# Two layers and 32 experts on one core: where the second layer's weights are split, and which expert weights come earlier

## The chip, the cores and the metric

The kernel runs on one core of one Trainium2 chip. Its time is device microseconds (us) of one execution. The core has TensorE (PE; its weight loads are a row of their own, PEld), VectorE (DVE), ScalarE (ACT), GpSimd (POOL) and SyncE (SP), which issues the DMAs here. A DMA is spread over 16 DMA engines.

## The reference, cut to what matters

256 tokens of width 1024 pass through two layers. Everything is float32.

- Layer one: norm, one wide projection, a windowed mean, a stick-breaking attention, a cross attention over a memory, three sigmoid gates, an output projection with a residual, then a feed-forward part of width 2816.
- Layer two: norm, `h @ w_in` (columns for two attentions, an index and two gates), block attention `a`, attention `b` on the 64 best-scored positions, `sigmoid(ga) * (o_a @ w_proj_a) + sigmoid(gb) * (o_b @ w_proj_b)`, then `@ w_out` and the residual.
- A mixture of experts behind it:

```
g_sel = argmax(h @ w_group + b_group)                 # one of 4 groups per token
e_logit = (h @ w_expert + b_expert)[group g_sel]      # 8 experts in it
top_p, top_i = top_k(softmax(e_logit), 2)             # 2 experts per token
hid = silu(xb @ w1[e]) * (xb @ w3[e]);  y = hid @ w2[e]
out = x + sum of gate * y;  then a last rms_norm with g_final
```

Each of the 32 experts has three matrices of 2 MB (w1, w3: 1024 x 512, w2: 512 x 1024), and all of them are read: about 201 MB of the 309 MB that the kernel moves.

## The kernel before, in words

**Units.** The dense weights of both layers come in 96 pieces ("units", numbered u) of 1 MB (128 partitions x 2048 floats). To keep float32 accuracy each is split: ACT copies it to a rounded high part (`w_hi`, line 1526), DVE subtracts that from the raw unit and writes the low part (`w_lo`, line 1867), and PE makes three products (lines 927 to 929). Raw, high and low parts have three places each, used in turn by u % 3. The raw places are `ring`, slots 1 to 3 of a 12-slot `arena` (one slot holds 1 MB). Unit u is loaded (`load`, line 685) once the low part of unit u - 3 is written. Layer two's units are `kiwi` (u = 65), `qi`, `kb`, `qb`, `vb`, `ka`, `qa`, `va`, eight `gate2`, four merges (`w_proj_a`, `w_proj_b`, u = 88 to 91) and four `out2` (92 to 95).

**The queue of DMAs.** SP issues all loads in one written order; each `wait_ge` holds back all that stands behind it. Expert weights are put between the units and behind them, each as soon as its place is free. `expert_load` (line 746) loads a whole matrix, `half_load` (753) a half of expert 0's, `chunk_load` (757) some chunks of a matrix (w1 and w3 have 8 chunks of 256 KB, w2 has 4 of 512 KB).

**Places of experts.** Expert e = 0 uses `even_w` (arena slots 8-9, the place of `x_both`, slots 4-5), e = 1 `odd_w` (w1 in slots 10-11, w3 in slots 0-1, w2 in slots 2-3), e = 2 `third_w` (where the last units are split), e = 3 `fourth_w`; expert 4's w1 has `next_w1`, its w3 follows into even w1's place. So odd w3's second half and w2 lie in the raw places of units, and wait for the last units.

**From the last unit to the experts.** After unit 95 PE computes the last routing logits (line 1234), then runs `CHOICE_WARM` = 7 products on ones whose result is not used (`keep_warm`, line 1117), then spreads the final norm's gain over the partitions (line 1348; ACT copies it to `final_row`, line 1798). DVE meanwhile chooses the experts (up to line 2402, `route_sel`). PE waits for that and for the first copy (`final_taken`), ranks the tokens (1354, 1356), gathers them for a quad of four experts (`first_collect`, 1380) and starts expert 0: w1 and w3 (line 1454), the gates' spread (1417), w2 (1480), and the sum into the tokens (`add_to_tokens`, 1433). The signals `e_w1_half` (expert 0's w1 half used), `e_w1`, `e_up` (w3 used) and `e_y` (w2 used) free the places, for which SP waits.

**Quads.** Quads 0 and 1 are written out on PE, quads 2 to 7 are a loop (`pe.Fori`, line 1490) with even and odd places alone. ACT has quad 0 written out and loops over 1 to 7. In the loop the last expert's w2 comes in two pieces (SP line 844), 1.5 MB and 0.5 MB; PE waits for the second ahead of its last quarter. Then the last norm follows (lines 1830 to 1838, 2504 to 2527).

Of the kernel before, what the change touches and what calls it, by code (L numbers as in the profile page):

```python
# [51 lines left out]
CHOICE_WARM = 7  # L52
# [231 lines left out]
def layers_kernel(nc, a, table, windows, out):  # L284
# [121 lines left out]

    def split_place(u):

        return split_at + 2 * SLOT_B * (u % 3)
# [50 lines left out]
    final_row = moe("final_row", [P, D])  # L460
# [95 lines left out]
    next_in = sem("next_w1_in")  # L556
# [4 lines left out]
    e_w1, e_w1_half = sem("e_w1"), sem("e_w1_half")  # L561
# [116 lines left out]
    def _(sp):  # L678
        def load(u):
            if u >= 3:  # L680
                sp.wait_ge(lo_ready, u - 2)
            kc, cols = units[u]["kc"], units[u]["cols"]
            dst = ring[:, u % 3, 0:kc * cols].rearrange("p (c n) -> p c n", c=kc)
            for c0, c1, src in units[u]["src"]:
                sp.dma_start(dst[:, :, c0:c1], src).then_inc(landed[u % 3], 16)
# [73 lines left out]
        for u in range(S2 + 3 * (NF - 2), U):  # L759
# [16 lines left out]
            load(u)  # L776
            if u == first["kiwi"]:
# [20 lines left out]
        expert_load(2, third_w, 2, in_third3[2])  # L798
        sp.wait_ge(route_T, 4)
# [122 lines left out]
    def _(pe):  # L922
# [8 lines left out]
        def unit(u):  # L931
# [3 lines left out]
            lo = w_lo[:, s, 0:kc * cols].rearrange("p (c n) -> p c n", c=kc)  # L935
# [409 lines left out]
        for half in range(2):  # L1345
            for j in range(4):
                c = 44 + 4 * half + j
                last = mm(ps[:, 4 + half, P * j:P * j + P], vec[:, c:c + 1].to_broadcast([P, P]), ident, start=True,
                          stop=True)
            last.then_inc(final_spread, 1)  # L1350
        pe.wait_ge(route_sel, 1)
        pe.wait_ge(final_taken, 1)

# [5 lines left out]
        def quad_body(q):  # L1359
# [24 lines left out]
            if not looped and q == 0:  # L1384
                pe.wait_ge(hot_part, 2)
                first_collect(4, (0, 1), xg_half)
                pe.wait_ge(final_taken, 2)
# [50 lines left out]
            for e in range(QUAD):  # L1438
                places, landing, arrived = place_of(e)
                done = pe.snap(e0 + e) if looped else e0 + e  # L1440
                for n in range(2):
                    if not looped and e == 0 and (q == 0 or n == 1):
                        pe.wait_ge(first_half[n], 16 * (q + 2 - n))
                    if not looped and (q, e, n) == (0, 1, 1):
                        pe.wait_ge(second_up_half, 16)
                    pe.wait_ge(landing[n], arrived[n])
                    for c in range(KC):
# [3 lines left out]
                        elif e == 0 and n == 0 and c % 4 == 0:  # L1451
                            pe.wait_ge((xg_part, xg_ready)[c // 4], q + 2)
                        for g in range(4):
                            last = mm(ps[SLOTS * g:SLOTS * g + SLOTS, 6, P * n:P * n + P],  # L1454
                                      xg[:, c, SLOTS * e:SLOTS * e + SLOTS], places[n][:, c, P * g:P * g + P],
                                      start=c == 0, stop=c == KC - 1, tile_position=(0, SLOTS * g))
                        if not looped and (e, n, c) == (0, 0, KC // 2 - 1):
                            if q == 0:
                                last.then_inc(e_w1_half, 1)
# [29 lines left out]
        quad_body(1)  # L1489
        with pe.Fori(2, n_pass * (EXPERTS // QUAD)) as q:  # L1490
            quad_body(q)
# [3 lines left out]
    def _(act):  # L1495
# [24 lines left out]
        def split_one(u):  # L1520
# [5 lines left out]
            fn(w_hi[:, u % 3, 0:n], ring[:, u % 3, 0:n], ACT.Copy).then_inc(hi_ready, 1)  # L1526
# [269 lines left out]
        for half in range(2):  # L1796
            act.wait_ge(final_spread, half + 1)
            fn(final_row[:, 512 * half:512 * half + 512], ps[:, 4 + half, :], ACT.Copy).then_inc(final_taken, 1)
# [4 lines left out]
        def quad_body(q):  # L1803
            e0 = act.snap(q * QUAD) if not isinstance(q, int) else 0
            act.wait_ge(xg_half, q + 2)
            if isinstance(q, int):
# [749 lines left out]
```

## Time and profile before

| | us |
|---|---|
| median of 3 runs (lowest, highest) | 1057.65 (1056.35, 1058.83) |
| the profiled execution | 1058.77 |
| its span, first to last instruction | 1056.7 |
| PE busy in it | 918.5 (87%) |
| DVE, ACT busy | 498.0, 385.2 |

How to read it: the span is cut in stretches, and each stretch has its own limit. "Idle before, releaser" names what ended an engine's idle time; "issue" is idle time for which the profile shows no event that was waited for. "us to landing" of a DMA runs from its issue on SP to the last of its pieces. PEclk is the granted TensorE clock as a share of 2.4 GHz. Packets of the queues named "instruction" fetch an engine's code. The profiled execution is 2.1 us longer than its span and 1.1 us longer than the median.

### The profile page before, as it was taken

How to read it: one execution, taken by the hardware profiler on the slowest of the kernel's cores; microseconds unless marked ns; L12 is line 12 of the kernel's file. 1: busy time of each engine (PE TensorE's matmuls, PEld its weight loads, DVE VectorE, ACT ScalarE, POOL GpSimd, SP SyncE). 2: the span in 40 equal slices, each digit the busy share in tenths (PEclk: the TensorE clock that was granted, in tenths of full speed). 3: DMA queues.
4: the chain of work that ended last, by engine and by line, in shares of the span. 5: the costliest groups of instructions: out<-in, count | busy, mean ns of one | idle time of the engine just before them, and what ended most of it. 6: DMA issues, size and time to landing. Idle time of an engine off the chain costs nothing.

```text
span 1056.7 us, 22572 instructions
## 1 busy us (share of the span) xinstructions
PE 918.5 (87%) x9950; PEld 761.6 (72%) x9950; DVE 498.0 (47%) x807; ACT 385.2 (36%) x553; POOL 21.6 (2%) x24
## 2 busy tenths in 40 slices
PE   9999999999999999999999997787757667575764
PEld 8998887888888888988777885665635546463643
DVE  5646768677676767889887650111100101010101
ACT  5445766464444446756666340000000000000001
POOL 0000002110000000000000000000000000000000
PEclk9999999999999999999999999999898978888987
DMA  9864445545655575665447999999999999999994
GB/s 328 293 194 159 165 136 175 163 150 190 213 162 195 199 254 162 198 202 163 160 170 286 389 401 426 425 425 421 427 427 427 430 429 427 429 427 428 431 428 200
DMA packets 89455, 309.49 MB, mean 293 GB/s; under 512 B 7940, under 2 KB 48696, under 8 KB 76600
## 3 DMA queue, kind: packets, MB, share of 16 engines
q1 hardware_dynamic: 88768, 308.40, 75.8%
q8 instruction: 42, 0.69, 0.3%
q10 hardware_dynamic: 632, 0.29, 0.1%
q14 instruction: 13, 0.11, 0.0%
HBM read 307.63 MB, written 1.05 MB: 292 GB/s over the span
## 4 chain that ended last, share of the span: by engine, by line
PE 62%; DMA 28%; DVE 4%; issue 3%; ACT 1%; POOL 0%; SPq 0%; DVEq 0%; ACTq 0%
DMA arena<-in_w 27%; PE ps L927 12%; PE ps L929 11%; PE ps L928 11%; PE ps L1037 7%; PE ps L1454 7%; PE ps L1041 4%; PE ps L1480 2%; DMA arena<-in_w_in 1%; PE ps L1219 1%; PE ps L1371 1%; DVE w_split L1867 1%; PE ps L1433 1%; PE ps L1417 1%; PE ps L1207 0%
## 5 line engine op out<-in xcount | busy, mean ns | idle before, releaser
L1867 DVE TENSOR_TENSOR w_split<-arena,w_split 128x2048 fp32r<-128x2048 f32 (+1 forms) x69 | 157.2, 2288 | 29.9 <-ACT w_split L1526 29.4
L1454 PE MATMUL ps<-arena,xg 128*32 128x128 f32 x2688 | 104.8, 318 | 74.0 <-DMA arena<-in_w 66.7
L2474 DVE TENSOR_TENSOR hid<-silu_e,ps 128x128 f32<-128x128 f32 x32 | 12.1, 378 | 311.7 <-ACT silu_e L1814 311.7
L1526 ACT ACTIVATE w_split<-arena 128x2048 fp32r<-128x2048 f32 x70 | 132.8, 1901 | 63.7 <-PE ps L929 53.1
L1454 PEld LDWEIGHTS ps<-arena,xg 128*32 128x32 f32 x2688 | 89.3, 129 | 91.8 <-DMA arena<-in_w 79.4
L927 PE MATMUL ps<-w_split,x_both 128*128 128x512 f32 x256 | 102.1, 399 | 0.6 <-DVE expo_pair L2117 0.6
L929 PE MATMUL ps<-w_split,x_both 128*128 128x512 f32 x256 | 99.8, 390 | 0.0
L928 PE MATMUL ps<-w_split,x_both 128*128 128x512 f32 x256 | 99.8, 390 | 0.0
L1814 ACT ACTIVATE silu_e<-ps 128x128 f32<-128x128 f32 x32 | 8.9, 277 | 240.1 <-PE ps L1454 240.1
L1037 PE MATMUL ps<-x_both,w_split 128*128 128x512 f32 x352 | 83.9, 390 | 0.1
L1480 PE MATMUL ps<-arena,hid_T 128*32 128x256 f32 x896 | 61.5, 415 | 24.1 <-DMA arena<-in_w 21.8
L1037 PEld LDWEIGHTS ps<-x_both,w_split 128*128 128x128 f32 x352 | 65.2, 188 | 13.3 <-issue 0.3
L927 PE MATMUL ps<-x_both,w_split 128*128 128x256 f32 (+1 forms) x256 | 73.0, 285 | 0.9 <-ACT p_tok L1561 0.8
L928 PE MATMUL ps<-x_both,w_split 128*128 128x256 f32 (+1 forms) x256 | 72.3, 283 | 0.0
L929 PE MATMUL ps<-x_both,w_split 128*128 128x256 f32 (+1 forms) x256 | 72.3, 283 | 0.0
L927 PE MATMUL ps<-w_split,o_hi 128*128 128x512 f32 (+1 forms) x176 | 68.0, 387 | 0.5 <-DVE gates L2090 0.5
L928 PE MATMUL ps<-w_split,o_hi 128*128 128x512 f32 (+1 forms) x176 | 67.0, 381 | 0.0
L1877 DVE TENSOR_TENSOR w_split<-arena,w_split 128x2048 fp32r<-128x2048 f32 x24 | 55.0, 2292 | 25.4 <-ACT w_split L1536 24.2
L929 PE MATMUL ps<-w_split,o_lo 128*128 128x512 f32 (+1 forms) x176 | 66.9, 380 | 0.0
L1480 PEld LDWEIGHTS ps<-arena,hid_T 128*32 128x32 f32 x896 | 30.3, 116 | 49.7 <-issue 30.9
L927 PEld LDWEIGHTS ps<-w_split,x_both 128*128 128x128 f32 x256 | 48.1, 188 | 14.2 <-issue 3.0
L929 PEld LDWEIGHTS ps<-w_split,x_both 128*128 128x128 f32 x256 | 48.0, 188 | 10.3
(325 smaller groups left out, 1462.0 us busy)
## 6 DMA issues: line engine op xcount, KB each, us to landing
arena<-in_w SPq DMA_DIRECT2D x65, 2048.0 KB, 26.3
arena<-in_w_in SPq DMA_DIRECT2D x41, 1024.0 KB, 5.2
even_w<-in_w SPq DMA_DIRECT2D x12, 2048.0 KB, 27.0
arena<-in_w_ffn_in SPq DMA_DIRECT2D x22, 1024.0 KB, 5.1
third_w<-in_w SPq DMA_DIRECT2D x6, 2048.0 KB, 16.9
arena<-in_w_ffn_out SPq DMA_DIRECT2D x11, 1024.0 KB, 4.9
arena<-in_w_out SPq DMA_DIRECT2D x8, 1024.0 KB, 6.2
extra_w<-in_w SPq DMA_DIRECT2D x4, 2048.0 KB, 19.0
```

Source lines behind the costliest of these rows:

```text
L927: mm(dst, l_hi, r_hi, start=start, stop=False)
L928: mm(dst, l_hi, r_lo, start=False, stop=False)
L929: return mm(dst, l_lo, r_hi, start=False, stop=stop)
L1037: mm(ps[:, bank + n, :], hi[:, c, P * n:P * n + P], x_both[:, c, :, :].rearrange("p a b -> p (a b)"), start=c == 0, stop=False)
L1041: last = mm(ps[:, bank + n, 0:T], lo[:, c, P * n:P * n + P], x_hi[:, c, :], start=False, stop=c == KC - 1)
L1219: mm(o[:, 0:T], v[:, 0, :], r[:, 0:T], start=True, stop=False)
L1454: last = mm(ps[SLOTS * g:SLOTS * g + SLOTS, 6, P * n:P * n + P], xg[:, c, SLOTS * e:SLOTS * e + SLOTS], places[n][:, c, P * g:P * g + P], ...
L1480: last = mm(ps[SLOTS * g:SLOTS * g + SLOTS, 7, 0:UC], hid_T[:, SLOTS * b:SLOTS * b + SLOTS], places[2][:, b, UC * g:UC * g + UC], start=b ...
L1526: fn(w_hi[:, u % 3, 0:n], ring[:, u % 3, 0:n], ACT.Copy).then_inc(hi_ready, 1)
L1867: v.tensor_tensor(w_lo[:, u % 3, 0:n], ring[:, u % 3, 0:n], w_hi[:, u % 3, 0:n].bitcast(F32), ALU.subtract).then_inc(lo_ready, 1)
L1877: v.tensor_tensor(w_lo[:, s, :], ring[:, s, :], w_hi[:, s, :].bitcast(F32), ALU.subtract)\
L2474: v.tensor_tensor(hid[:, :].rearrange("p (b i) -> p i b", b=4), silu_e[:, :].rearrange("p (i b) -> p i b", b=4), ps[:, 6, P:2 * P].rearran ...
```

## The change

1. From unit 65 on the raw unit lands in the place of its low part, and DVE subtracts in place. There are four such places in turn by u % 4: the three of `w_lo` and `ring_low` (arena slot 3). For one turn in four the raw unit lands in arena slot 3 itself, as for the others it lands in its `w_lo`. Unit u is now loaded once unit u - 4 has been computed (`unit_done`) and the high part of u - 3 is written. Arena slots 1 and 2 are free of units from there on.
2. The 2 MB of expert 1 that lie in slots 1 and 2 are loaded there: w3's second half behind unit `ka` (74), w2's first half behind unit `qa` (76). W2's second half (slot 3) waits for unit 92.
3. `spare_w` (4 KB per partition, 0.5 MB) takes the first two chunks of expert 4's w3, loaded behind unit 95. The next two chunks go where expert 0's first two w1 chunks were, once these are used (`e_w1_part`, after chunk 1 instead of chunk 3). The other half goes as before, at `e_w1`. `final_row` moves to `next_w1`'s place.
4. The spread of the final gain moves on PE from ahead of the ranking to behind quad 1, and its copies on ACT likewise; ACT has quad 1 written out too. `CHOICE_WARM` goes from 7 to 23.
5. In the looped quads PE runs `keep_warm(10)` ahead of the last expert's w1 and again ahead of its w3.

```
-CHOICE_WARM = 7
+CHOICE_WARM = 23
+LAST_WARM = 10
+    ring_low = nc.alloc_sbuf_tensor_at("ring_low", [P, UNIT], F32R, offset=arena_at + 3 * SLOT_B)
+    raw_low = [nc.alloc_sbuf_tensor_at(f"raw_low{i}", [P, UNIT], F32, offset=split_at + 2 * SLOT_B * i + SLOT_B)
+               for i in range(3)]
+    def low_place(u):
+        if u < KW:
+            return w_lo[:, u % 3, :]
+        turn = (u - U) % 4
+        return w_lo[:, turn - 1, :] if turn else ring_low[:, :]
+    def raw_place(u):
+        if u < KW:
+            return ring[:, u % 3, :]
+        turn = (u - U) % 4
+        return raw_low[turn - 1][:, :] if turn else ring[:, 2, :]
...
         def load(u):
-            if u >= 3:
+            turn = (u - U) % 4
+            if u >= KW + 4:
+                sp.wait_ge(unit_done, u - 3)
+                sp.wait_ge(hi_ready, u - 2)
...
+            elif u >= 3:
                 sp.wait_ge(lo_ready, u - 2)
...
             load(u)
+            if u == first["ka"]:
+                sp.wait_ge(lo_ready, KW)
+                chunk_load(1, odd_w, 1, slice(KC // 2, KC), landed_w[1][1])
+            elif u == first["qa"]:
+                chunk_load(1, odd_w, 2, slice(0, 2), second_up_half)
...
         expert_load(1, odd_w, 0, landed_w[1][0])
-        sp.wait_ge(lo_ready, U - 2)
-        chunk_load(1, odd_w, 1, slice(KC // 2, KC), landed_w[1][1])
+        sp.wait_ge(unit_done, U - 3)
+        chunk_load(1, odd_w, 2, slice(2, 4), landed_w[1][2])
         sp.wait_ge(unit_done, U - 2)
         expert_load(2, third_w, 0, in_third3[0])
-        sp.wait_ge(lo_ready, U)
-        expert_load(1, odd_w, 2, landed_w[1][2])
         sp.wait_ge(unit_done, U - 1)
         expert_load(2, third_w, 1, in_third3[1])
         sp.wait_ge(unit_done, U)
         expert_load(2, third_w, 2, in_third3[2])
+        sp.dma_start(spare_w[:, :, :], sources[1][:, 4, 0:2, :]).then_inc(spare_in, 16)
...
         expert_load(3, fourth_w, 1, in_fourth[1])
-        for half, landing in ((0, first_half[1]), (1, landed_w[0][0])):
-            sp.wait_ge((e_w1_half, e_w1)[half], 1)
-            chunk_load(4, next_w, 1, slice(KC // 2 * half, KC // 2 * half + KC // 2), landing)
+        sp.wait_ge(e_w1_part, 1)
+        sp.dma_start(even_w[0][:, 0:2, :], sources[1][:, 4, 2:4, :]).then_inc(first_half[1], 16)
+        sp.wait_ge(e_w1, 1)
+        chunk_load(4, next_w, 1, slice(KC // 2, KC), landed_w[0][0])
...
         keep_warm(CHOICE_WARM, 5)
-        for half in range(2):
-            for j in range(4):
-                ... (the spread of the final gain, 8 products; now behind quad_body(1))
         pe.wait_ge(route_sel, 1)
-        pe.wait_ge(final_taken, 1)
...
                 for n in range(2):
+                    if looped and e == QUAD - 1:
+                        keep_warm(LAST_WARM, 5)
...
         quad_body(1)
+        (the spread)
+        pe.wait_ge(final_taken, 2)
         with pe.Fori(2, n_pass * (EXPERTS // QUAD)) as q:
```

## Rows read from the trace of the kernel before

**Rows 1.** The page: busy tenths in 40 slices of PE and DMA.

```profile
PE   9999999999999999999999997787757667575764
DMA  9864445545655575665447999999999999999994
```

**Rows 2.** Windows: busy us (instructions) of each engine, PEclk, DMA share, GB/s.

```profile
400.00:440.00 40.00, 39.27 (x310) 36.24 (x309) 32.21 (x49) 28.07 (x46) 1.96 (x3) 1.00 0.57 183
628.00:632.00 4.00, 4.00 (x115) 3.38 (x109) 2.28 (x8) 0.88 (x2) 0.00 (x0) 1.00 1.00 354
760.00:1035.00 275.00, 181.98 (x3752) 138.74 (x3744) 23.66 (x63) 17.92 (x47) 0.00 (x0) 0.87 1.01 428
```

**Rows 3.** The chain that ended last, 1000 to 1057: start, us, what.

```profile
1011.19 2.00 PE ps L1454 x64
...
1013.21 27.31 DMA arena<-in_w
...
1040.56 3.46 PE ps L1454 x64
...
1045.13 1.98 PE ps L1480 x32
```

**Rows 4.** Timeline of ACT: start, us, engine, line, operation; the split of unit 83.

```profile
504.54 1.91 ACT L1526 ACTIVATE w_split<-arena 128x2048 fp32r<-128x2048 f32 x1 [2.95 <-PE ps L929]
```

**Rows 5.** Timeline of SP's issues, 586 to 627.

```profile
586.26 0.34 SPq L746 DMA_DIRECT2D extra_w<-in_w  x1
...
604.90 8.09 SPq L746 DMA_DIRECT2D third_w<-in_w  x2
615.66 0.33 SPq L746 DMA_DIRECT2D extra_w<-in_w  x1
623.99 3.43 SPq L757 DMA_DIRECT2D arena<-in_w  x2
```

**Rows 6.** DMA issues at 558.69, 615.66, 627.09 and 1020.14: KB each, us to landing.

```profile
even_w<-in_w SPq DMA_DIRECT2D x1, 1024.0 KB, 5.0
...
extra_w<-in_w SPq DMA_DIRECT2D x1, 2048.0 KB, 12.3
...
arena<-in_w SPq DMA_DIRECT2D x1, 1024.0 KB, 8.9
...
arena<-in_w SPq DMA_DIRECT2D x1, 512.0 KB, 25.3
```

**Rows 7.** Timeline around the choice of experts.

```profile
615.77 1.81 PE L1117 MATMUL ps<-ones 128*128 128x128 f32 x14
617.41 1.95 PE L1348 MATMUL ps<-tab,vec 128*128 128x128 f32 x16
618.45 0.20 DVE L2402 TENSOR_SCALAR chosen<-left_e 128x64 f32<-128x64 f32 x1
```

**Rows 8.** Windows ahead of and in the last expert's w1 (as rows 2).

```profile
1032.80:1035.60 2.80, 0.00 (x0) 0.00 (x0) 0.00 (x0) 0.38 (x1) 0.00 (x0) 1.00 1.02 432
1035.60:1038.60 3.00, 2.65 (x64) 2.19 (x64) 0.00 (x0) 0.00 (x0) 0.00 (x0) 0.69 0.95 397
```

**Rows 9.** Windows between idle times of PE called issue, and one loop pass (814.03).

```profile
642.30:648.80 6.50, 3.90 (x128) 3.63 (x128) 0.00 (x0) 0.38 (x1) 0.00 (x0) 1.00 0.98 416
705.55:708.20 2.65, 2.17 (x28) 1.14 (x28) 0.00 (x0) 0.38 (x1) 0.00 (x0) 1.00 1.00 427
814.03:873.47 59.44, 40.46 (x804) 31.05 (x808) 5.21 (x14) 3.83 (x10) 0.00 (x0) 0.85 1.01 429
```

**Rows 10.** The chain, 620 to 720: an idle time called issue.

```profile
704.59 0.96 issue
```

**Rows 11.** DMA queues, 558 to 760, then 760 to 1050: packets, MB, share of 16.

```profile
q8 instruction: 22, 0.36, 0.7%
...
q1 hardware_dynamic: 8393, 120.03, 97.3%
q14 instruction: 1, 0.01, 0.0%
```

More of the change, by code:

```diff
@@ L404, in layers_kernel @@
     gates2 = temp("gates2", [P, 16, T])
+    KW = next(u for u, x in enumerate(units) if x["name"] == "kiwi")
+    ring_low = nc.alloc_sbuf_tensor_at("ring_low", [P, UNIT], F32R, offset=arena_at + 3 * SLOT_B)
[11 more added lines that the diff above has]
+        return raw_low[turn - 1][:, :] if turn else ring[:, 2, :]
     def split_place(u):
@@ L1452, in quad_body @@
                             pe.wait_ge((xg_part, xg_ready)[c // 4], q + 2)
+                        source = places[n][:, c, :]
+                        if not looped and (q, e, n) == (1, 0, 1) and c < KC // 2:
+                            source = (spare_w if c < 2 else even_w[0])[:, c % 2, :]
                         for g in range(4):
                             last = mm(ps[SLOTS * g:SLOTS * g + SLOTS, 6, P * n:P * n + P],
-                                      xg[:, c, SLOTS * e:SLOTS * e + SLOTS], places[n][:, c, P * g:P * g + P],
+                                      xg[:, c, SLOTS * e:SLOTS * e + SLOTS], source[:, P * g:P * g + P],
                                       start=c == 0, stop=c == KC - 1, tile_position=(0, SLOTS * g))
+                        if not looped and (q, e, n, c) == (0, 0, 0, 1):
+                            last.then_inc(e_w1_part, 1)
                         if not looped and (e, n, c) == (0, 0, KC // 2 - 1):
                             if q == 0:
-                                last.then_inc(e_w1_half, 1)
                                 first_collect(7, (4, 5), xg_done)
@@ L1489, in _ @@
         quad_body(1)
+        for half in range(2):
+            for j in range(4):
+                c = 44 + 4 * half + j
+                last = mm(ps[:, 4 + half, P * j:P * j + P], vec[:, c:c + 1].to_broadcast([P, P]), ident, start=True,
+                          stop=True)
+            last.then_inc(final_spread, 1)
+        pe.wait_ge(final_taken, 2)
         with pe.Fori(2, n_pass * (EXPERTS // QUAD)) as q:
@@ L1803, in quad_body @@
         def quad_body(q):
-            e0 = act.snap(q * QUAD) if not isinstance(q, int) else 0
+            e0 = act.snap(q * QUAD) if not isinstance(q, int) else q * QUAD
             act.wait_ge(xg_half, q + 2)
-            if isinstance(q, int):
+            if isinstance(q, int) and q == 0:
                 fn(xg[:, 2:4, :].rearrange("p a b -> p (a b)"), ps[:, 5, 0:2 * P], ACT.Copy).then_inc(xg_part, 1)
@@ L1823, in _ @@
         n_pass = act.value_load(passes_i[0:1, 0:1], min_val=1, max_val=T // SLOTS)
-        with act.Fori(1, n_pass * (EXPERTS // QUAD)) as q:
+        quad_body(1)
+        for half in range(2):
+            act.wait_ge(final_spread, half + 1)
+            fn(final_row[:, 512 * half:512 * half + 512], ps[:, 4 + half, :], ACT.Copy).then_inc(final_taken, 1)
+        with act.Fori(2, n_pass * (EXPERTS // QUAD)) as q:
             quad_body(q)
```

33 lines of the change are left out of this document (17 added, 16 removed).

## The prediction, made before the change was run

> **What bounds the kernel now.** The page's slices come first [rows 1]: PE is at nine tenths or more up to slice 23, about 610 us, and then falls to 7 and 4; the DMA row does the reverse, 4 to 6 before and 9 from slice 22 on. So there are two kernels. Up to the last unit PE sets the pace and the DMA engines have room (share 0.57 from 400 to 440). From 760 to 1035 they move 428 GB/s at share 1.01 and PE is busy 182 of 275 us [rows 2]: 2 MB (2.10 million bytes) take 2.10 / 0.428 = 4.9 us, and a load more or less in this stage is worth that. The seam between them is the place to look at. From 628 to 632 the rate is 354, not 428 [rows 2]: the queue nearly runs out just after the experts are chosen, because all places are full. The end is read from the chain [rows 3]: the last w3 lands at 1040.5, PE takes 3.46 us for its 64 instructions (the same 64 took 2.00 at 1011), and w2 follows at 1045.13.
>
> **The change part by part.** The sum is made against the profiled execution, 1058.77 us (span 1056.7). That is 1.1 above the median of the runs, 1057.65, and the result is carried over to the median by that difference.
>
> *Units loaded later.* Unit u - 3's low part no longer lets unit u in; unit u - 4's end on PE does. The tightest split in the middle is that of unit 83: ACT began it at 504.54, having waited 2.95 us for PE [rows 4], and its load would now go out one unit before, where a 1 MB load onto a free queue takes 5.0 [rows 6]; a unit takes about 1.05 / 0.183 = 5.7 us by the rate from 400 to 440 [rows 2]. It is just in time, and PE needs the unit only two units later, 11 us, for two splits of some 2 us each. At the other end unit 95 goes out with the wait that now releases the first expert load behind it, at 586.26 [rows 5], and ahead of that in the queue: landing near 592. PE wants it when unit 94 ends, at 604.90, where third w3 is issued [rows 5]. Its cover is PE's own work on units 93 and 94; were the load 8 us late, PE would wait. Cost 0; bounds 0 and +1 us.
>
> *2 MB of expert 1 early.* Two 1 MB loads go out near 445 and 458, into a queue at share 0.57 [rows 2]: free. What is late next? If the queue stayed full, the end would come 4.9 us sooner. It doesn't. All that is issued up to 615.66 landed at 615.66 + 12.3 = 628.0 [rows 5, 6]. Without 2 MB the queue has run dry by the time unit 95 ends: third w2, the 0.5 MB of `spare_w` and fourth w3 (4.5 MB, 11.0 us) can't flow before 604.90 + 8.09 - 0.33 = 612.7 [rows 5] plus about 2.5 (5.0 for 1 MB [rows 6], less 2.45 of transfer), so they end near 626. Then 0.5 MB at `e_w1_part`, and nothing until `e_w1`. The gain ends at a new gap, and what decides is when the `e_w1` load goes out and lands.
>
> *The ranking later.* Before, 7 warm products are 14 PE instructions in the 1.64 us from 615.77 to 617.41, and the 8 products of the spread end at 619.36 [rows 7]. After, 23 warm products stand there: 46 instructions at 1.64 / 14 = 0.117 are 5.4 us, at the 0.111 of the fastest stretch 5.1; PE is free at about 620.9 to 621.1. DVE had its choice at 618.65 [rows 7]: the warm products, not the choice, hold the ranking. It comes 1.6 us later, and the chain from there to expert 0's w1 is serial. All instructions count: 16 products more, 8 gone. The spread itself, 1.95 us on PE and two copies on ACT, moves behind quad 1. PE then waits for ACT's second copy before quad 2, and nobody waits for PE but loads that have several others ahead of them in the queue (a load at the end takes 25.3 us to land for 4.9 of its own [rows 6]): 0, bound +0.5.
>
> *The `e_w1` load.* Before: issued at 627.1 (the second of two from 623.99 on, 3.43 us in all), landed 8.9 later, at 636.0 [rows 5, 6]. After: issued at 627.1 + 1.6 = 628.7 onto a dry queue, landed 5.0 later, at 633.7 if nothing else is on the engine. That is 2.3 sooner. An instruction packet may fall on the last engine: 22 packets had 0.7% of 16 engines' 202 us, 1.03 us each [rows 11]. So 1.3 to 2.3 sooner, and 0.8 if a packet holds up half as much again (1.5, an estimate for what waits behind it); I take 1.6. The 1 MB loaded in the gap (`spare_w` and the `e_w1_part` chunk) is what buys this. From here the queue is never empty again, as before, and each landing follows the last by 4.9 us. Bounds: -2.4, and +1.2 if the gap costs as much as the bytes bring in.
>
> *The warm products in the loop.* Ahead of the last w1 PE stood idle from 1032.8 to 1035.6, and w1 then ran at a granted clock of 0.69, which is a mix of 1.2 and 2.4 GHz [rows 8]; w3 behind it took 3.46 us instead of 2.00. Ten products (2.2 us at the full clock) fit in either gap: w3 lands at 1040.5 [rows 3], w1 4.9 before it, at 1035.6. If they keep the clock up, w3 ends 1.46 us sooner. Not all of it counts: w2's last 0.5 MB land at 1020.14 + 25.3 = 1045.4 [rows 6], the 1.5 MB ahead of them 1.2 before, at 1044.2. W2 would start at 1044.2 instead of 1045.13, and its last quarter is then ready. Gain 0.9; bounds 1.4 and a loss of 2.9 (below).
>
> *Code.* Nothing else is on the path: `spare_w`'s wait is met long before, ACT's written-out quad runs in slack of many us.
>
> Sum: -1.6 - 0.9 = -2.5. 1058.77 - 2.5 = 1056.3 on the scale of the profiled execution, 1055.2 on that of the median.
>
> **A page's rule against this change.** PE's instructions come in blocks, and the trace shows where they end. Between two idle times of PE called issue it ran 128 + 128 instructions [rows 9], and a packet of the instruction queue is 0.36 MB / 22 = 16 KB [rows 11]: 256 instructions are one block. One such idle time ends at 705.56 [rows 10]; 56 instructions of PE and PEld and two more of its queue later, at 708.2, the looped quad starts [rows 9]. A pass has 804 + 808, with its branch 1613. It starts at 58 in a block and ends at 1671, in the seventh (1536 to 1792). After 760 there is no packet of that queue, though the loop is passed five times more [rows 11]: seven blocks, and the next one fetched ahead, all stay. After the change the 16 added warm products put the start at about 121 (four instructions each), the 20 in the loop add 80, and the end is at 121 + 1693 = 1814: 22 instructions into an eighth block, with a ninth fetched ahead. Whether nine fit, no row shows.
>
> The Trainium skill (Runtime: NRT & Kernel Launch, Instruction fetch mechanics) says that PE's instruction memory is a FIFO of 128 KiB, 2048 instructions, refilled in 16 KiB blocks. By that rule eight blocks are all, the ninth drives out the first, and each pass fetches anew. The block size agrees with the trace; the depth isn't shown beyond eight.
>
> **The rivals.**
> 1. *The loop's code no longer stays.* For it: the count above. Against it: nothing in the rows but that eight blocks do fit. Price: 9 blocks in each of 5 passes, 45 packets of 1.03 us beside full queues. Spread over 16 engines that is 2.9 us on each, over eight 5.8, and with the estimate of 1.5 us for a packet's whole delay 8.5. The end waits for the slowest engine. I take 8.5: 1055.2 + 8.5 = 1063.7. It decides once the body reaches an eighth block.
> 2. *The gap takes everything.* PE reaches `e_w1` 1.6 later and the dry queue restarts no earlier than the old one flowed, with the tail's 0.9 alone: 1056.8. For it: the old queue still moved 354 GB/s in the gap [rows 2], 83% of the full rate, and the ranking is 1.6 us late. Against: the old load took 8.9 us, a free queue takes 5.0.
> 3. *The warm products are in the way.* If the clock stays at 1.2 GHz in the last expert, ten take 4.5 us: w1 3.3, warm 4.5 from 1035.66 end at 1043.4, 2.9 behind the landing of w3. Then 1057.65 - 1.6 + 2.9 = 1059.0. For it: 0.69 in [rows 8]. Against: PE is then hardly idle ahead of w1, and the clock was at full before it fell there.
> 4. *The whole 2.5 MB pays*, with no gap: -6.1 - 0.9, 1050.6. For it: only that the bytes are free. Against: all places are full until expert 0's w1 is used.
>
> **How the numbers follow.** My forecast has 0.50, rival 1 0.22, rival 2 0.14, rival 3 0.07, rival 4 0.07. A measurement of this kernel tells a change of some 0.2%, 2.1 us, from none: faster is below 1055.5. The forecast's own range is 1053.4 to 1057.2, two thirds of it on the faster side: 0.34; with rival 4, 0.41. Same: 0.16 of the forecast, rival 2, and 0.03 of rival 3, 0.33. Slower: rival 1 and the rest of 3, 0.26. The range goes from 1052.6 to 1064.5: it leaves out rival 4 and the upper part of rival 1.
>
> **What would show it.** The ranking on PE at about 621 instead of 619.3, right behind the warm products; a dip in the DMA rate near 613 and a deeper one, to nearly nothing, between 626 and 631; the `e_w1` load issued near 628.7 and landed by 635; every later landing of the same load earlier by about 1.6; in the tail w3's 64 instructions in 2.0 us and the last w2 starting on its landing, not on `hid_T`. Wrong it is if the 16 KB instruction packets go on after 760 (rival 1), if the last landing is not earlier than 1045.4 (rival 2), if the clock around 1036 to 1044 is 0.5 with PE busy at 1040.5 (rival 3), or if PE shows new idle time before 612 that ends with a DMA or with `w_split`.

## The result: 1082.6 us, 2.4% slower

The changed kernel took 1082.60 us in the median of 5 runs (1080.34 to 1083.93), the kernel before 1057.63 beside it (5 runs, 1056.35 to 1058.83). The ratio is 1.0238, 95% interval 1.0227 to 1.0250. The forecast was 1055.2 with a range up to 1064.5: wrong in its sign, and outside the range.

The profiled execution of after took 1083.93 us with a span of 1082.0, 25.3 above the span of before. Its page, the busy tenths of PE and DMA, the granted clock, and the row of the instruction queue (packets, MB, share of 16 engines):

```profile
PE   9999999999999995999999998788766776766665
...
PEclk9999999999999996999999999999798988988899
DMA  9864444546565535666447989999999999999994
...
q8 instruction: 88, 1.44, 0.5%
```

Against [rows 1] two things are new. PE has a hole in slice 15, about 406 to 433 us, where it had nine tenths; its clock falls there too. And the instruction queue moved 88 packets instead of the 42 of the kernel before (the same row is shown for e12 below).

The windows that answer to [rows 2] (the last one starts a little later, since the stream does), and the hole by itself:

```profile
400.00:440.00 40.00, 26.81 (x178) 23.67 (x178) 20.33 (x34) 20.75 (x34) 1.97 (x3) 0.79 0.62 206
403.00:417.00 14.00, 1.14 (x10) 0.94 (x9) 3.46 (x7) 4.71 (x10) 0.55 (x1) 0.71 1.02 355
...
761.00:1051.00 290.00, 202.77 (x4088) 165.36 (x4091) 25.41 (x68) 18.55 (x48) 0.00 (x0) 0.90 1.01 425
```

PE lost 12.5 us of its 39.3 in the first window. In the last one the queues are as full as before and the rate is 425 instead of 428 GB/s.

**The 25.3 us by stretch.** All times are from one profiled execution of each kernel. "Landing" is the time at which the slowest of the 16 DMA engines has finished a load. The fourth column is a mended kernel, explained under e12.

| stretch | before | after | e12 |
|---|---|---|---|
| last unit done by PE | 612.64 | 628.58 (+15.9) | 613.20 |
| from there to the landing of the `e_w1` load | 23.37 | 21.27 (-2.1) | 20.78 |
| from there to the last landing | 409.43 | 421.73 (+12.3) | 410.88 |
| from there to the end of the span | 11.26 | 10.4 (-0.9) | 10.4 |

The second and the fourth line are the gains that the forecast counted (1.6 and 0.9). The first it priced at nothing. The third holds the spread, priced at nothing too, and the loop's code, which was no term of the sum but rival 1.

**The first loss: 15.9 us at the feed-forward's end.** The timeline of SP in after (start, us until the last of the group, line, what is loaded), and of the waits from 390 to 440 (engine, operation, what it waited for: us in total, times, longest):

```profile
397.76 0.99 SPq L717 DMA_DIRECT2D raw_low<-in_w_in  x2
398.79 0.89 SPq L789 DMA_DIRECT2D next_w<-in_w  x1
400.10 0.34 SPq L720 DMA_DIRECT2D gain_row<-in_g_ffn  x1
403.20 1.80 SPq L717 DMA_DIRECT2D raw_low<-in_w_in  x2
```

```profile
ACT w_split L1569 <- DMA raw_low<-in_w_in: 18.1, 2, 9.1
PEld ps L1160 <- DVE h L2003: 13.8, 2, 13.0
PE ps L1160 <- DVE h L2003: 13.2, 2, 12.9
DVE y_tok L2026 <- ACT junk L1734: 10.1, 1, 10.1
```

The text on the change above says that a unit from 65 on waits for the computing of unit u - 4. For the first four of them that isn't so. Their wait is a branch of `load` of its own:

```
            elif u >= KW and turn:
                sp.wait_ge(unit_done, max(v for v in range(KW) if v % 3 == turn - 1) + 1)
                sp.wait_ge(hi_ready, u - 2)
            elif u >= KW:
                sp.wait_ge(lo_ready, KW)
                sp.wait_ge(hi_ready, u - 2)
```

Units 65 and 66 are the first whose raw weights land in a low place. Such a place is free only when PE is done with the unit that has it: units 63 and 64, at 397.7 and 403.2. Before, the same two loads went out once the low parts of units 62 and 63 were split, at 381.4 and 385.3, 16 and 18 us sooner. Behind the first of them SP issues 2 MB of `next_w` and a gain row, and unit 66 follows those. ACT works in order. It waits 9.1 us for unit 65 and 8.9 for unit 66, and the feed-forward's norm stands behind that split on ACT:

```profile
402.04 1.11 ACT L1569 ACTIVATE w_split<-raw_low 128x1088 fp32r<-128x1088 f32 x1 [9.15 <-DMA raw_low<-in_w_in]
412.07 1.91 ACT L1569 ACTIVATE w_split<-raw_low 128x2048 fp32r<-128x2048 f32 x1 [8.91 <-DMA raw_low<-in_w_in]
413.89 0.58 ACT L1734 ACTIVATE junk<-ps 128x512 f32<-128x512 f32 x1
```

DVE waits for `junk`, PE for `h`, idle for 12.86 us until 416.92, and then the granted clock is 0.81 from 417 to 440, a mix of the two levels. Unit 65 is done at 429.6 instead of 413.6. From there to the last unit nothing is lost and nothing regained (199.0 us in both kernels).

**The second loss: the loop's code is fetched again in every pass.** The timeline of PE at a loop head, and its waits from 774 to 1069:

```profile
771.65 1.15 PE L1461 MATMUL ps<-y_part,gate_T 32*128 32x256 f32 x16 [0.50 <-ACT y_part L1859]
778.45 2.92 PE L1400 MATMUL ps<-one_hot,n3g 128*128 128x128 f32 x12 [5.65 <-issue]
```

```profile
PE ps L1400 <- issue: 27.0, 5, 5.7
...
PE ps L1445 <- issue: 8.4, 5, 1.9
PE ps L1489 <- issue: 8.2, 5, 2.0
```

L1400 is the first operation of the looped quad. Five times PE has no instruction there for 5.4 us in the mean, and ten times more, for 1.7 in the mean, further on in the loop; in e2, whose code stays, it has no such idle time. The queue in that stretch, 44 packets where [rows 11] has none:

```profile
q8 instruction: 44, 0.72, 1.0%
```

This is the first rival: the loop starts at 121 of one block, ends 22 instructions into its eighth, and is fetched anew in each of five passes, nine packets a pass. PE's own stalls did not slow the loads: the first DMA engine (of the 16, the one that is done first with a load) finishes the last load 318.18 us after its first landing of this stage (742.00 to 1060.18), exactly as before (720.49 to 1038.67). The packets cost more: the slowest engine ends 11.4 us after the first instead of 6.8. At the stage's start that distance was 1.9 us against 5.2 before, so it grew by 9.5 instead of 1.6. Of the fifteen profiles here only those of after and e1, the two with 88 packets, end with 11.4; the other thirteen have 2.3 to 6.9. That it is the packets which hold up the slower engines is inferred from this; no row shows on which engine a packet ran.

**The third loss: the queue runs dry at the loop's start.** PE's timeline between quad 1 and the loop, against [rows 9, 10]:

```profile
725.24 1.15 PE L1461 MATMUL ps<-y_part,gate_T 32*128 32x256 f32 x16 [0.47 <-ACT y_part L1859]
726.31 2.05 PE L1529 MATMUL ps<-tab,vec 128*128 128x128 f32 x16
729.32 3.83 PE L1400 MATMUL ps<-one_hot,n3g 128*128 128x128 f32 x32 [0.95 <-ACT final_row L1867]
```

The spread and ACT's second copy put 3.0 us between quad 1 and the loop. The first load that the loop releases went out 21.2 us later than before (735.1 against 713.9): 15.9 from the units, 1.7 from the ranking, 3.0 from the spread, and 0.6 that none of them explains. What was left in the queue landed only 17.6 us later (732.9 against 715.3 on the first engine), so the first engine's landings lie 9.1 us apart there, where before they lay 5.2 apart and elsewhere in the stream lie 4.9. The slowest engine's lie 6.95 apart instead of 4.89, so 2.1 us are lost there.

### The profile page after: what moved, and what is told of

It is laid out like the page before. It is cut to its first block, busy times and chain, and to the rows that moved or that the text cites. A ratio compares the mean times of both kernels' runs of the same rounds, so it can differ in the third digit from the quotient of the medians.

```text
span 1082.0 us, 23140 instructions
## 1 busy us (share of the span) xinstructions
PE 944.1 (87%) x10222; PEld 791.4 (73%) x10222; DVE 497.9 (46%) x807; ACT 385.6 (36%) x553; POOL 21.7 (2%) x24
## 4 chain that ended last, share of the span: by engine, by line
PE 68%; DMA 18%; issue 6%; DVE 5%; ACT 2%; POOL 0%; SPq 0%; DVEq 0%; ACTq 0%
DMA arena<-in_w 16%; PE ps L964 12%; PE ps L965 11%; PE ps L966 11%; PE ps L1074 7%; PE ps L1489 6%; PE ps L1516 5%; PE ps L1078 4%; PE ps L1400 3%; PE ps L1445 1%; DMA arena<-in_w_in 1%; PE ps L1461 1%; PE ps L1154 1%; DMA raw_low<-in_w_in 1%; PE ps L1256 1%
## 5 line engine op out<-in xcount | busy, mean ns | idle before, releaser
L1489 PE MATMUL ps<-arena,xg 128*32 128x128 f32 x2672 | 86.0, 277 | 30.7 <-DMA arena<-in_w 16.5
L1569 ACT ACTIVATE w_split<-arena 128x2048 fp32r<-128x2048 f32 x46 | 87.8, 1912 | 44.5 <-PE ps L966 37.3
L1489 PEld LDWEIGHTS ps<-arena,xg 128*32 128x32 f32 x2672 | 74.2, 111 | 40.3 <-DMA arena<-in_w 20.5
L964 PE MATMUL ps<-w_split,x_both 128*128 128x512 f32 x256 | 102.1, 399 | 0.6 <-DVE expo_pair L2161 0.6
L966 PE MATMUL ps<-w_split,x_both 128*128 128x512 f32 x256 | 99.8, 390 | 0.0
L1911 DVE TENSOR_TENSOR w_split<-arena,w_split 128x2048 fp32r<-128x2048 f32 x38 | 87.3, 2312 | 25.1 <-ACT w_split L1569 25.0
L965 PE MATMUL ps<-w_split,x_both 128*128 128x512 f32 x232 | 90.4, 390 | 0.0
L1074 PEld LDWEIGHTS ps<-x_both,w_split 128*128 128x128 f32 x352 | 65.2, 188 | 13.3 <-issue 0.3
L964 PE MATMUL ps<-x_both,w_split 128*128 128x256 f32 (+1 forms) x256 | 73.9, 288 | 0.9 <-ACT p_tok L1604 0.9
L965 PE MATMUL ps<-x_both,w_split 128*128 128x256 f32 (+1 forms) x256 | 73.2, 286 | 0.0
L964 PE MATMUL ps<-w_split,o_hi 128*128 128x512 f32 (+1 forms) x176 | 68.1, 387 | 0.5 <-DVE gates L2134 0.5
L1921 DVE TENSOR_TENSOR w_split<-arena,w_split 128x2048 fp32r<-128x2048 f32 x24 | 55.0, 2293 | 25.4 <-ACT w_split L1579 24.2
L966 PE MATMUL ps<-x_both,w_split 128*128 128x256 f32 x224 | 64.0, 286 | 0.0
L965 PE MATMUL ps<-w_split,o_hi 128*128 128x512 f32 (+1 forms) x168 | 63.9, 380 | 0.0
L1400 PE MATMUL ps<-one_hot,n3g 128*128 128x128 f32 x224 | 36.9, 340 | 28.3 <-issue 27.3
L964 PEld LDWEIGHTS ps<-w_split,x_both 128*128 128x128 f32 x256 | 48.0, 188 | 14.2 <-issue 3.3
## 6 DMA issues: line engine op xcount, KB each, us to landing
arena<-in_w SPq DMA_DIRECT2D x64, 2048.0 KB, 25.3
```

The costliest lines, as they stand in the source:

```text
L964: mm(dst, l_hi, r_hi, start=start, stop=False)
L965: mm(dst, l_hi, r_lo, start=False, stop=False)
L966: return mm(dst, l_lo, r_hi, start=False, stop=stop)
L1074: mm(ps[:, bank + n, :], hi[:, c, P * n:P * n + P], x_both[:, c, :, :].rearrange("p a b -> p (a b)"), start=c == 0, stop=False)
L1400: last = mm(ps[:, 4 + half, P * i:P * i + P], n3g[:, tb, 4 * half + i, :], one_hot[:, tb, :], start=tb == 0 and i == 0, stop=tb == 1 and i ...
L1569: fn(w_hi[:, u % 3, 0:n], raw_place(u)[:, 0:n], ACT.Copy).then_inc(hi_ready, 1)
```

## The experiments

Each kernel is the changed one with the edit shown. From e5 to e9 the kernel of e4 is the base (`CHOICE_WARM` at 7, and `KW` as in e4 unless another is given), for e10 and e11 it is that of e9. Times are medians with the ratio to the kernel before on the same chip.

**e1, the four low places from four units later.** With `KW` at 69 instead of 65 the feed-forward's end has three places again.

```
-    KW = next(u for u, x in enumerate(units) if x["name"] == "kiwi")
+    KW = next(u for u, x in enumerate(units) if x["name"] == "kiwi") + 4
```

> The change, but the four low places take raw units from unit 69 on instead of 65, so that units 65 to 68 are loaded as before the change. Theory A (in the change units 65 and 66 are let in by PE's end of units 63 and 64, 16 us later than before; ACT, which must split them in order, holds up the squares of the feed-forward's end, and PE stands still for 12.9 us): all of it goes, 1082.6 - 16 = 1066.6 us, and PE ends its last unit near 613 instead of 628.6. Rival (the raw unit in the low place, with the subtraction in place, is what is slow): some 27 of 31 units still do that, so it stays within 2 us of 1082.6.

1069.33 us (4 runs), ratio 1.0115 [1.0093, 1.0136]: 13.3 less. The last unit is done at 614.96, not 628.58; the instruction queue still has 88 packets. The first loss is shown, and that it is apart from the second. In this profiled execution 2.3 us of it stay.

**e2, seven warm products ahead of the ranking, and e3, none in the loop.** Both shorten PE's code, at different places: e2 puts the loop's end at 213 of its seventh block, e3 at 197 (offsets from 0, good to a few instructions).

```
e2:  -CHOICE_WARM = 23   +CHOICE_WARM = 7
e3:  -LAST_WARM = 10     +LAST_WARM = 0
```

> The change with 7 instead of 23 warm products ahead of the choice: PE's code ahead of the loop is 64 instructions shorter, the loop is the same. Theory B (the loop's end lies 22 instructions in an eighth block of 256, so with the block fetched ahead nine are wanted and eight stay): now the loop ends in its seventh block, no 16 KB instruction packets after the loop's first pass, 46 fewer in all, 8 us less for them and 1.6 us less for the earlier ranking: about 1073. Rival (the 20 warm products in each pass are what holds the loop up, by their own time): the packets may be as they are, and the time falls by the ranking's 1.6 us at most, 1081.

> The change without the 20 warm products in each pass of the loop: 80 instructions fewer in the loop, which then ends in its seventh block. Theory B: the repeated packets go, 8 us less, but the tail's 0.9 us come back: 1075.5. Rival (the warm products' own time): also lower, by what they take, so this run alone does not part the two; the pair with the run before it does. If neither holds, the repeated packets stay and the time is 1083.

e2: 1071.97 us (4 runs), 1.0137 [1.0115, 1.0158]. e3: 1073.63 us (4 runs), 1.0156 [1.0136, 1.0176]. Both have 42 packets and no idle time at a loop head. But e2 still has the 20 products of each pass and e3 the 23 ahead of the ranking, so the packets go with where the loop lies and not with the products by themselves. The waits of PE from 774 to 1045 in e2 are all for data:

```profile
PE ps L1489 <- DMA arena<-in_w: 39.1, 21, 2.9
PE ps L1516 <- DMA arena<-in_w: 23.8, 19, 1.9
PE ps L1489 <- DMA even_w<-in_w: 12.7, 8, 2.9
PE ps L1461 <- ACT y_part L1859: 2.0, 4, 0.5
```

e3 leaves the ranking and the spread as they are and gives 9.0 us back, although its tail is longer again (11.2 us from the last landing to the end). With those 0.85 the code's share is some 9.8 us, an estimate from one difference. e2 gives 10.6: the code, and the ranking 1.6 us sooner. In e2 no landing of the first engine lies more than 4.95 from the last at the loop's start, in e3 one is 7.5 away: the spread alone does not empty the queue there, the spread with the late ranking does. The late ranking without the spread was not run.

**e4, both mended**, `KW` at 69 and `CHOICE_WARM` at 7.

> Units from 69 on and 7 warm products. Theory: 16 + 8 + 1.6 us off, 1057.0 us, about the kernel before (1057.6): the 2 MB loaded early are worth little, because the queue then runs dry until expert 0's w1 is used, and what is left of the difference is the tail's 0.9 us less and a gap of the DMA engines at the loop's start (the spread behind quad 1) of some 2 us more. Rival (the early 2 MB pay in full once nothing is in the way): 4.9 us below that, 1052.

1058.62 us (10 runs), ratio 1.0008 [0.9998, 1.0019]; run again beside e12 (as e13) 1058.01 (11 runs), 1.0006 [0.9997, 1.0015]. Two edits take 24 of the 25 us away. After, e1, e2 and e4 are the four combinations of the two edits: `KW` is worth 13.3 us without the other edit and 13.4 with it, `CHOICE_WARM` 10.6 and 10.7 (after on another chip, where the kernel before took 1057.63 against 1057.24 here). The two losses add up and do not touch each other. What is left is "no change", where gains of some 3 us had been counted.

> The kernel of e4 again, on the same chip as e12, so that the two are compared there: 1058.0 to 1059.5 by its first run (1058.6). Theory: 2 to 3.5 above e12. Rival: equal to it.

**e5, e6 and e7, where the loop lies.** Is it the number of blocks, the length of the code, or an address? N small products ahead of the loop push it along without changing it.

```
+        for _ in range(N):          # 10 in e5, 12 in e6, 52 in e7
+            mm(ps[:, 6, 0:16], ones, ones[:, 0:16], start=True, stop=True)
         pe.wait_ge(final_taken, 2)
         with pe.Fori(2, n_pass * (EXPERTS // QUAD)) as q:
```

> The kernel of e4 (1058.6) with ten small products (16 columns) on PE ahead of the looped quad. Blocks of 256 instructions, counted from the idle times of PE at their ends: the loop now runs from 97 of block 35 to 253 of block 41, three instructions short of an eighth block. Theory (the loop's code stays as long as it lies in seven blocks): instruction packets as in e4 (42), none after the loop's first pass, 1058.5 to 1060. Rival (the larger code by itself, or the place of the loop's start, costs): some 2 to 4 us more than e4.

> The same with twelve products instead of ten: the loop ends 5 instructions into block 42, its eighth. Theory: the packets come back in every pass, about 88 in all, PE idles near 5.9 us at the head of every pass, and the time is 1058.6 + 8 = 1066 to 1069 for two products more. Rival (what cost in the kernel after was the number of warm products, not the block's border): as with ten products, 1059.

> The same with fifty-two products: the loop runs from 9 of block 36 to 165 of block 42, again in seven blocks, though it ends further on than with twelve. Theory: 42 to 44 packets, none after the first pass, and 1059 to 1062 (the forty products more are some 160 instructions in the gap ahead of the loop, up to 3 us). Rival (a fixed address or the whole length of the code decides): 88 packets or more, 1067 or more.

| kernel | loop, block and offset | packets | us, runs | ratio |
|---|---|---|---|---|
| e4 | 35:57 to 41:213 | 42 | 1058.62, 10 | 1.0008 [0.9998, 1.0019] |
| e5 | 35:97 to 41:253 | 42 | 1058.01, 10 | 1.0005 [0.9995, 1.0015] |
| e6 | 35:105 to 42:5 | 43 | 1058.90, 10 | 1.0020 [1.0002, 1.0037] |
| e7 | 36:9 to 42:165 | 43 | 1073.45, 4 | 1.0145 [1.0128, 1.0162] |
| after | 35:121 to 42:21 | 88 | 1082.60, 5 | 1.0238 [1.0227, 1.0250] |

Blocks are numbered over the whole program, and the places come from the instructions counted between the idle times at block ends; offsets count from 0 and are good to a few instructions. e6 is a miss of my theory. Its loop reaches offset 5 of an eighth block, and the profiled execution fetched nothing in the later passes. So a loop that touches eight blocks can stay. In after, whose loop runs 16 instructions further into the same block, all of them are fetched again; the nearest reading is that PE has by then asked for a ninth, which drives the first out. The times of the packets bear it out. The 43rd, by this count the first behind the eighth block, comes at 773.4 in after, at the end of the first pass and before the next begins at 778.4, and the refetch follows from 775.8 on. In e6 it comes at 1049.6, when the passes are over or nearly so. No run shows the point between 5 and 21 at which PE asks. e6's runs spread more than e5's (1056.6 to 1065.0 against 1056.3 to 1060.6), and whether some of them fetched again was not profiled.

The Trainium skill (Runtime: NRT & Kernel Launch, Instruction fetch mechanics) gives PE a FIFO of 128 KiB, filled in blocks of 16 KiB: eight blocks. By that rule e6 keeps its loop and after loses it as soon as a ninth block is fetched, and both traces agree. The same section of the Trainium skill calls the cost of a block's border mostly hidden. In this loop it was not: some 9 to 10 us.

e7 is a second miss, of price. Its code stays (43 packets, none in the later passes, though its loop ends further on than after's), so an address or the length of the program is not what decides. But its time is 15 us above e5. The timeline of PE in e7:

```profile
705.17 2.05 PE L1529 MATMUL ps<-tab,vec 128*128 128x128 f32 x16
707.06 19.53 PE L1533 MATMUL ps<-ones 128*128 128x16 f32 x104
726.43 5.75 PE L1400 MATMUL ps<-one_hot,n3g 128*128 128x128 f32 x32
```

Fifty-two products took 19.5 us, 0.19 for each of 104 instructions, where I had counted up to 3 us for forty of them. At the price of e5 (20 instructions in 2.30 us, 0.115 each) the 104 would be 12.0; the rest is the clock, granted at 0.57 in this stretch, a mix of 1.2 and 2.4 GHz near the lower:

```profile
707.10:726.50 19.40, 19.40 (x107) 19.40 (x105) 0.00 (x0) 0.60 (x1) 0.00 (x0) 0.57 0.56 235
```

The first load of the loop went out at 734.1, the queue ran dry (the first engine's landings lie 24.5 us apart), and 15.4 of the 17.2 us that the products take beyond those of e5 reached the end. That is the third loss in large: the start of the loop has some 2 us of slack.

**e8 and e9, the four low places from unit 72 and from unit 71.** In its profile e4's last unit is still 4.3 us late, in that of e13 3.0. Both profiles show the slowest of their kernel's runs (1061.28 of a median of 1058.62, 1062.23 of 1058.01), so the typical run may be less late.

```
e8:  ... if x["name"] == "kiwi") + 7
e9:  ... if x["name"] == "kiwi") + 6
```

> The kernel of e4 with the four low places from unit 72 on instead of 69. The first unit of the new order now takes the new place, not one whose unit is still to be used, and units 73 and 74 wait for units 69 and 70 (before: done at 437.5 and 444.3), no later than they used to. Theory (what e4 still loses, 4.3 us at the last unit, is loads 69 to 71 waiting for units 66 to 68): last unit done near 612.7, and 1054.5 to 1056, faster than the kernel before by some 2 us. Rival (e4's late last unit comes from elsewhere, the chip or the 2 MB beside the units): 1058 to 1059.

> The kernel of e4 with the four low places from unit 71 on (e4: 69, e8: 72). Worked out from the trace of before: each first load of the new order goes out when its place's last user is done or split, and lands 5.2 us later; against the start of its split in before that is 11.3 and 11.0 us late for units 65 and 66 in the kernel after, 3.1, 2.9 and 3.1 late for 69 to 71 in e4, 4.1 late for unit 72 in e8, and with the change at 71 only 3.1 late for unit 71. Theory (PE's lost time ahead of the last unit is ACT waiting in order for such a load): last unit done 612.7 to 614.7 instead of 617.0, time 1054.5 to 1057. Rival (the late last unit comes from elsewhere): 617 and 1058.6.

e8: 1059.32 us (10 runs), 1.0016 [1.0006, 1.0025], last unit 617.09. e9: 1060.53 us (6 runs), 1.0029 [1.0017, 1.0041], last unit 615.61. Neither helps; my theory's number for e8 was wrong, and the working for e9 (a load 3.1 us late) was right in the lateness and wrong in what it costs. The waits of e9 from 426 to 458, ACT's and then PE's:

```profile
ACT w_split L1569 <- DMA raw_low<-in_w_in: 2.9, 1, 2.9
ACT rope_turned L1587 <- PE ps L966: 2.8, 2, 1.7
...
PE ps L1363 <- ACT head_score L1803: 2.1, 1, 2.1
```

Two splits in a row wait for their loads, unit 71's for 2.9 us and unit 72's for 2.4, and `head_score` stands behind the second on ACT. The timelines of ACT, e9 and then before:

```profile
437.61 1.91 ACT L1569 ACTIVATE w_split<-raw_low 128x2048 fp32r<-128x2048 f32 x1 [2.87 <-DMA raw_low<-in_w_in]
...
444.36 1.91 ACT L1569 ACTIVATE w_split<-arena 128x2048 fp32r<-128x2048 f32 x1 [2.38 <-DMA arena<-in_w_in]
446.30 0.87 ACT L1803 ACTIVATE head_score<-ps 128x384 f32<-128x384 f32 x2
```

```profile
439.98 1.92 ACT L1526 ACTIVATE w_split<-arena 128x2048 fp32r<-128x2048 f32 x1
441.93 0.87 ACT L1760 ACTIVATE head_score<-ps 128x384 f32<-128x384 f32 x2
```

PE idles 2.1 us where before it had no idle time at all (unit 71 done at 454.10, before 451.12). In e4 and e8 the same wait is 1.7 and 2.0 us, and the granted clock from 445 to 450 is 0.73 in e8. At each of the three starts tried (69, 71, 72) some load changes from waiting for a split to waiting for a unit, and between 435 and 450 a delay of 3 us has nothing to hide it.

The stretch from unit 65's end to unit 71's shows this in all fifteen profiles. It takes 37.5 us in the five that have no change of order in it (before, after, e2, e3, e12), and 38.4 to 42.9 in the ten that have one. From unit 71 to the last it takes 161.5 us with three places (before, e12) and with four (after, e4, e9): the four places cost nothing but their beginning. Kernels with the same start differ by 3 us, though (e9 39.9, e10 42.9), so that single profiles can't rank the starts 69, 71 and 72.

**e10, e9 without the warm products in the loop, and e11, e9 without the 2 MB early** (`LAST_WARM = 0`; the two loads of expert 1 moved behind its w1, at the last units).

> The kernel of e9 without the ten products ahead of the last expert's w1 and w3. The code of both lies in seven blocks, so this is the tail alone. Theory: from the last landing to the end 11.2 us instead of 10.4, the time 0.8 us longer than e9. Rival (they do nothing where the code fits): the same.

> The kernel of e9 with expert 1's 2 MB loaded in the last units again, behind its w1, and not beside units 74 and 76. Theory (the gap ahead of the e_w1 load takes the rest): the e_w1 load lands 1 to 2.5 us later against the last unit, and the time is 1 to 2.5 us longer than e9. Rival (the 2 MB are worth nothing, since the queue runs dry before e_w1 anyway): the same. Second rival (they are worth their whole transfer): 4.9 us longer.

e10: 1060.87 us (8 runs), 1.0028 [1.0018, 1.0039]. e11: 1060.92 us (6 runs), 1.0030 [1.0018, 1.0042]. By time neither can be told from e9 (1.0029). The profile of e10 has the tail at 11.2 us against 10.4 in e9, as forecast; the medians differ by 0.3, within what runs differ. All profiles agree on the tail: 10.4 us in the twelve with the ten products, 11.2 in the three without. In e11 the `e_w1` load lands 22.3 us after the last unit against 20.5 in e9, and the time does not show that either. Nor is that distance the same in two profiles of one kernel: 20.6 in e4, 23.1 in e13. The size of both gains rests on profiled executions alone.

**e12, the units as before and the rest of the change.** Three low places throughout, the 2 MB in the last units again, w2's first half behind the split of unit 95; `spare_w`, the chunk at `e_w1_part`, the spread behind quad 1 and ten products in the loop stay, `CHOICE_WARM` is 7.

```
-    KW = next(u for u, x in enumerate(units) if x["name"] == "kiwi")
+    KW = U
...
-            if u == first["ka"]: ... chunk_load(1, odd_w, 1, slice(KC // 2, KC), landed_w[1][1])
-            elif u == first["qa"]: ... chunk_load(1, odd_w, 2, slice(0, 2), second_up_half)
+        sp.wait_ge(lo_ready, U - 2)    # behind expert 1's w1, as in the kernel before
+        chunk_load(1, odd_w, 1, slice(KC // 2, KC), landed_w[1][1])
```

> The kernel of e4 with all 97 units loaded and split as in the kernel before (three low places), and expert 1's 2 MB therefore in the last units again; the rest of the change stays (spare_w, the chunk at e_w1_part, the spread behind quad 1, ten products in the loop, CHOICE_WARM 7). Theory (the four low places cost 3 to 4.4 us ahead of the last unit wherever they begin, because ACT and DVE have no slack between 435 and 455): last unit done 612.6 to 613.0, time 1055.0 to 1057.0, faster than e4 by 2 to 3.5. Rival (something else in the change delays the units): last unit 615 or later, time 1058.6.

1056.81 us (11 runs), ratio 0.9994 [0.9985, 1.0003]: the only version whose median is not above the kernel before, and not shown to be below it. It is 1.2 us under e4 on the same chip (e13, 1058.01), less than the 2 to 3.5 expected. The intervals against the kernel before overlap, but the runs hardly do: ten of e12's eleven are at or below the lowest of e13's eleven (1057.49). The last unit is done at 613.20, and PE has no idle time between 426 and 458. The page of e12 has the same instruction queue as the kernel before, and its tail answers to [rows 3, 8]:

```profile
q8 instruction: 42, 0.69, 0.3%
```

```profile
1033.78 0.83 PE L1152 MATMUL ps<-ones 128*128 128x128 f32 x6
1035.08 1.95 PE L1487 MATMUL ps<-arena,xg 128*32 128x128 f32 x64 [0.46 <-DMA arena<-in_w]
1036.96 2.50 PE L1152 MATMUL ps<-ones 128*128 128x128 f32 x20
1039.99 1.95 PE L1487 MATMUL ps<-arena,xg 128*32 128x128 f32 x64 [0.53 <-DMA arena<-in_w]
1041.87 1.15 PE L1459 MATMUL ps<-y_part,gate_T 32*128 32x256 f32 x16
1043.74 1.93 PE L1514 MATMUL ps<-arena,hid_T 128*32 128x256 f32 x32 [0.72 <-DMA arena<-in_w]
```

w3 takes 1.95 us instead of 3.46, and w2 now starts on its landing. Of the 2.6 us gained at `e_w1` against the last unit, 1.5 are gone by the last landing (410.9 us instead of 409.4). They are almost all distance between the engines. The first engine takes 407.0 us from the one load to the other, before 406.8; the slowest is 2.5 us behind it at `e_w1` and 6.3 at the end, before 4.1 and 6.8. What sets that distance no run tells.

## Why the prediction was wrong, step by step

- *Units loaded later* (cost 0, bounds 0 and +1 us): **the step that failed**, at 15.9 us. Two units were looked at, 83 as the tightest "in the middle" and 95 at the end. The units at which the order changes, 65 to 68, were not. There unit 65 waits for unit 63 and unit 66 for unit 64 (u - 2, not u - 4), and their splits stand on ACT ahead of the feed-forward's norm, for which PE waits. The rule itself held where it was looked at: unit 83 keeps its place relative to its neighbours. The last condition named in the forecast (new idle time of PE before 612 that ends with `w_split` or a DMA) came true, by way of two other engines: PE's 12.9 us end with DVE's `h`, DVE's wait with ACT's `junk`, and ACT's wait in `w_split` with the DMA.
- *2 MB of expert 1 early*: free as bytes, as said. Worth nothing that the time can show (e11, e12), and it has a price that the step did not count, the beginning of the four low places: e12, without the four places and without the early load, is 1.2 us below the kernel of e4.
- *The ranking later* (1.6): right. The `e_w1` load goes out 16.11 us after the last unit instead of 14.44, +1.7. The timeline answers to [rows 7]:

```profile
631.70 5.38 PE L1154 MATMUL ps<-ones 128*128 128x128 f32 x46
636.92 0.33 PE L1383 MATMUL ps<-chosen,tab 128*128 128x64 f32 x2
```

- *The `e_w1` load* (-1.6, bounds -2.4 and +1.2): within its bounds in the profile; it was issued at 644.69 onto a nearly dry queue, landed 5.2 later, 2.1 sooner against the last unit. The kernel of e12 has 2.6 without the early 2 MB. But only the slowest engine gained: the first landed its part 20.4 us after the last unit, before 19.3, and e13 has the load no sooner than before (23.1 against 23.4). No time shows this term, so it is not shown to be worth 1.6 us at the end.
- *The spread behind quad 1* (0, bound +0.5): wrong. It put 3.0 us between two quads. The forecast named a cover, the loads ahead in the queue, and took its size from the end of the stream. At the start of the loop the cover is nearly nothing: the landings of the kernel before already lie 5.2 us apart there instead of 4.9. With the ranking 1.6 us late as well the queue runs dry (after, e3); without that it does not (e2, e4).
- *The warm products in the loop* (-0.9): right, -0.85.
- *Rival 1, the loop's code* (0.22, price 8.5): came true, at some 9 to 10 us by e3. The count of blocks was exact. That no row spoke against eight blocks was taken as evidence for the forecast; it said nothing about the ninth.

Rival 3 did not occur: the clock was 1.00 from 1061.8 to 1068.3. Nor did rival 4: no version came near 1050.6. Rival 2 (the gap takes everything, 1056.8) was not refuted. Once both losses are mended e4 took 1058.6, and e12, where the units are not late either, 1056.81, which is rival 2's price and not the forecast's 1055.2; e12 also has the ranking early, so it is no clean test of it. With rival 1 alone the time would have been near 1064 by its price, or 1067 by after's time without the units' 15.9 us; the units made it 1082.6.

## What to carry to other kernels

When a ring of buffers changes its order or its depth, work out the first turn of the new order unit by unit, each load's new release against the start of its consumer: e1 shows that this one seam was worth 13 us, while the steady state cost nothing. Before a difference of 2 or 3 us in a stretch is believed, look at a second profile of the same kernel. Count a looped body in instruction blocks, with its start offset, before adding anything to it or ahead of it, and treat the last block's edge as a cliff: here 16 instructions lie between no cost and 9 to 10 us. Where work is moved "behind" a stage, compute the slack there in us; a wait of an in-order engine costs what stands behind it, not what it is for.

## What the hardware showed unexpectedly

- Sixteen more instructions in an eighth block (e6 to after) separate 43 packets from 88 and a loop that is kept from one that is fetched in each pass; a PE without code stands for 5.4 us at each loop head beside full queues.
- Instruction packets do not slow the first DMA engine at all (318.18 us in both kernels, 318.2 to 318.3 in all fifteen profiles); they show as distance between the first and the slowest engine, 11.4 us instead of 6.8, and a consumer waits for the slowest.
- Products with 16 columns are no cheaper than those with 128: 0.115 us an instruction in e5 against 5.38 / 46 = 0.117 ahead of the ranking. And while PE ran 104 of them without a pause, the granted clock was 0.57 over 19.4 us (e7), for the most part the lower level.
